# The last strip's rows summed and turned one piece sooner, and a weight split held back, behind an output norm

## What is computed

```python
m = jnp.concatenate([a, p], axis=-1) @ w_o[l]
x = x + rms_norm_2(m, post_mix_g[l])
h = rms_norm_2(x, pre_ffn_g[l])
up = causal_dwconv(h @ w_up[l], conv_w[l], conv_b[l])
y = (jax.nn.gelu(up[..., :D_FF_2], approximate=True) * up[..., D_FF_2:]) @ w_down[l]
x = x + rms_norm_2(y, post_ffn_g[l])
```

## Time and profile before

| | |
|---|---|
| median of 3 runs | 2122.08 us (2122.01 to 2123.68) |
| profiled execution, its own time | 2123.21 us |
| its span (first to last instruction) | 2121.5 us |
| TensorE busy | 2112.6 us (100%) |
| VectorE, ScalarE, GpSimd busy | 1255.2 us, 1051.7 us, 190.1 us |
| weight load (beside the matmuls) busy | 1812.9 us |
| DMA | 194 GB/s in the mean |

### The profile page before, as it was taken

How to read it: one execution, slowest core, us unless ns; L and a number is a source line. 1 busy time by engine, 2 the same in 40 slices (tenths; PEclk the granted TensorE clock), 3 DMA queues, 4 the chain that set the end, 5 groups by cost and what they waited for, 6 DMA issues and landing times.

```text
span 2121.5 us, 26812 instructions
## 1 busy us (share of the span) xinstructions
PE 2112.6 (100%) x11014; PEld 1812.9 (85%) x11014; DVE 1255.2 (59%) x1337; ACT 1051.7 (50%) x1224; POOL 190.1 (9%) x90
## 2 busy tenths in 40 slices
PE   9999999999999999999999999999999999999998
PEld 8888888888888888888888888888888888888887
DVE  6555656656455555465667755576666644666565
ACT  6654555544334443344555645465455433455543
POOL 3000000000000000000004000002222100222210
PEclk9999999999999999999999999999999999999999
DMA  8565557665666666665676656655655666556663
GB/s 288 166 209 174 179 169 231 221 197 174 209 195 184 196 209 194 182 195 193 219 237 189 187 171 196 192 183 174 193 191 181 212 195 189 182 176 203 202 208 120
DMA packets 218923, 411.98 MB, mean 194 GB/s; under 512 B 13360, under 2 KB 22704, under 8 KB 218288
## 3 DMA queue, kind: packets, MB, share of 16 engines
q1 hardware_dynamic: 217936, 405.77, 60.5%
q10 hardware_dynamic: 864, 4.49, 0.6%
HBM read 403.92 MB, written 6.29 MB: 193 GB/s over the span
## 4 chain that ended last, share of the span: by engine, by line
PE 98%; DMA 1%; DVE 0%; ACT 0%; issue 0%; SPq 0%; DVEq 0%
PE ps L1491 98%; DMA xT<-in_x_dram 0%; DMA E<-passed_rows 0%; PE ps L1494 0%; DMA passed_rows<-xN 0%; DVE aHL L1248 0%; DVE xN L1258 0%; DVE T L1237 0%; SPq L858 0%; DVE Wl L1141 0%; ACT aHL L944 0%; DVE aHL L1241 0%; SPq L863 0%; ACT T L1070 0%; DVE Wl L1137 0%
## 5 line engine op out<-in xcount | busy, mean ns | idle before, releaser
L1141 DVE TENSOR_TENSOR Wl<-raw,Wh 128x1024 fp32r<-128x1024 f32 x743 | 911.4, 1246 | 648.3 <-ACT Wh L920 647.6
L1491 PE MATMUL ps<-aHL,Wh 128*128 128x512 f32 x3336 | 1159.1, 392 | 1.6 <-DVE Wl L1137 1.0
L920 ACT ACTIVATE Wh<-raw 128x1024 fp32r<-128x1024 f32 x743 | 767.4, 1054 | 583.3 <-PE ps L1491 580.7
L1491 PE MATMUL ps<-aHL,Wl 128*128 128x256 f32 x3328 | 930.1, 280 | 0.0
L1491 PEld LDWEIGHTS ps<-aHL,Wh 128*128 128x128 f32 x3336 | 623.9, 187 | 140.7 <-issue 1.1
L1491 PEld LDWEIGHTS ps<-aHL,Wl 128*128 128x128 f32 x3328 | 628.3, 189 | 0.5
L1491 PE MATMUL ps<-Wh,hid 128*128 128x512 f32 x1728 | 532.6, 389 | 0.0
L1491 PEld LDWEIGHTS ps<-Wh,hid 128*128 128x128 f32 x1728 | 324.3, 188 | 67.4
L1491 PE MATMUL ps<-Wl,hid 128*128 128x512 f32 x864 | 336.2, 389 | 0.0
L1491 PEld LDWEIGHTS ps<-Wl,hid 128*128 128x128 f32 x864 | 162.2, 188 | 33.6
L1491 PE MATMUL ps<-Wh,oHL 128*128 128x512 f32 x512 | 158.8, 390 | 0.0
(11 more groups left out here) (177 smaller groups left out, 796.2 us busy)
## 6 DMA issues: line engine op xcount, KB each, us to landing
raw<-in_mlp_w_dram SPq DMA_DIRECT2D x256, 512.0 KB, 4.2
raw<-in_w_up_dram SPq DMA_DIRECT2D x176, 512.0 KB, 3.7
raw<-in_sb_w_qkv_dram SPq DMA_DIRECT2D x93, 512.0 KB, 4.8
raw<-in_w_down_dram SPq DMA_DIRECT2D x88, 512.0 KB, 4.2
raw<-in_w_in_dram SPq DMA_DIRECT2D x64, 512.0 KB, 4.6
raw<-in_sb_w_o_dram SPq DMA_DIRECT2D x32, 512.0 KB, 5.3
raw<-in_w_o_dram SPq DMA_DIRECT2D x32, 512.0 KB, 4.3
passed_rows<-xN SPq DMA_DIRECT2D x16, 256.0 KB, 4.3
```

The lines of the kernel that those rows point to most:

```text
L920: e.activation(Wh[:, i % NW, :], rawv[:, i % NRAW, :], ACT.Copy).then_inc(st["hi"][0], 1)
L1141: e.tensor_tensor(Wl[:, i % NW, :], rawv[:, i % NRAW, :], Wh[:, i % NW, :].bitcast(F32), ALU.subtract).then_inc(st["lo"][0], 1)
L1491: return e.matmul(o, l, r, start=start, stop=stop, skip_group_check=True)
```

## The change

Two things are edited. In `evac_mixed`, `add_rows(3)` and `move_rows(3)` no longer stand in the put-off job `second_tiles` (iteration of piece 0), but in the evacuation itself, right behind `keep_last`, one iteration sooner. `turn_blocks` is put off by three iterations from there, so it also comes one iteration sooner, behind piece 2 and not behind piece 3; there it is registered ahead of `tiles(2)`. And the split that iteration 0 of the strip emitted (that of piece 4) moves to iteration 1.

```diff
@@ -498,11 +498,11 @@
             add_rows(1)
             p.pieces[p.at + 1]["early"] = dict(hi=st["t_hi"], lo=st["t_lo"], turning=tiles(0, (2, 3)))
             step("keep_last", set=s, row=st["mixed_row"], kept=kept[1])
+            add_rows(3)
+            move_rows(3, "ffn", added[3] * 2)
 
             def second_tiles():
                 tiles(1)
-                add_rows(3)
-                move_rows(3, "ffn", added[3] * 2)
                 add_rows(2)
             later(1, second_tiles)
             later(3, lambda: tiles(2))
@@ -678,7 +678,7 @@
     for i in range(N):
         q = p.pieces[i]
         p.at = i
-        while n_split <= (i + LEAD if i > 2 else i + 1):
+        while n_split <= (i + (LEAD - 1 if q["early"] else LEAD) if i > 2 else i + 1):
             split(n_split)
             n_split += 1
         need = []
```

## The result

| | median, us | lowest to highest | ratio to before, 95% interval |
|---|---|---|---|
| before, 8 runs | 2122.51 | 2122.0 to 2123.68 | |
| changed, 8 runs | 2128.66 | 2127.91 to 2129.74 | 1.0029 (1.0021 to 1.0038) |

The change makes the kernel 6.15 us, 0.29%, slower: clear of the 0.2% bound, if only just. Predicted were 2127.3 us, in a range from 2124.2 to 2130.2. The profiled execution of the changed kernel took 2127.91 us, its span is 2126.2 us, and its mean granted clock 0.998.

A forecast was written before the change was run, and what follows sets the result against it. TensorE bounds the kernel, busy 2112.6 of 2121.5 us, so only its waits and clock matter. +4.35 (wait) - 0.36 (old wait gone) + 1.2 (clock) = +5.2 us on 2122.08 gives 2127.3 us, range 2124.2 to 2130.2.

The forecast's parts named there:

- What the change can win: TensorE's wait for L1241 before piece 6, for tiles 12 and 13, goes away: 0.36 us saved.
- The order of the jobs as the cause: On ScalarE and VectorE the blocks' job now comes ahead of turning tiles 8 to 11, which delays piece 4: 4.35 us.
- The wait: TensorE before piece 4 waits for tiles 8 and 9: it starts at 1399.8 in place of 1395.45, 4.35 us.
- T: Start of the transposition L1237 on VectorE, which waits for the moved rows: 5.4 us after the first issue, 1395.4.
- piece 4 at T + 4.4: TensorE starts piece 4 4.4 us after the transposition starts, behind the blocks' halves and those of tiles 8 and 9.
- The clock: Clock falls 3.4 us into TensorE's wait; 2.4 us of matmuls at half speed lose 1.2 us, bounds 0 and 3.4.
- The held split: Piece 4's weight split comes later, ready at 1391.4 and wanted at 1395.45: covered by pieces 1 to 3, cost nothing.
- The sum ahead of tiles 4 and 5: On VectorE, low halves of tiles 4 and 5 still end before piece 2 wants them: cost nothing, 0.9 us to spare.
- The load behind the rows on SyncE: Piece 10's load goes out at about 1391.9, not 1386.96; its split waits past 1401 anyway: cost nothing.
- The clock that holds: Rival: TensorE's wait before piece 4 comes, but the clock doesn't fall: +4.0 us, 2126.1 us; chance 0.33.
- The quick transfer: Rival: rows land sooner, transposition at 1393.8, TensorE waits 2.75 us before piece 4: +2.4 us, 2124.5 us; chance 0.14.
- The other side: Rival: tiles 8 to 11 ready by 1395.45, no new wait, only 0.36 us saved: 2121.7 us; chance 0.08.

The follow-up runs named there:

- both reorderings: Two kernels, each the change with one edit: turning of tiles 8 to 11 registered ahead of the blocks (2122.63 us), or the blocks put behind piece 3 again (2122.48 us).
- the held split alone: The kernel before with only the changed `while` line, which holds back piece 4's weight split by one piece: 2122.79 us, before 2122.72, ratio 1.0001.
- the runs with the loads held: The change, with SyncE waiting until the moved rows have landed before it issues the next weight loads: 2129.04 us, before 2122.53; one more profiled execution took 2130.01.
- the runs with matmuls of ones: Matmuls of ones into an unused bank ahead of piece 4's wait: the change with 34 (2129.95 us) or 19 (2127.10), only the transposition ahead with 8 (2124.43).
- the move alone: The change with the old `while` line, so without holding back piece 4's split: 2130.47 us, before 2122.72, ratio 1.0042; a second, single profiled run took 2128.64 us.
- the change again: The change itself, unedited, timed and profiled a second time: 2130.10 us, before 2122.53, ratio 1.0033.
- the run with 19 matmuls of ones: The change, with 19 matmuls of ones into an unused bank just ahead of TensorE's wait for piece 4: 2127.10 us, before 2122.61, ratio 1.0022.
- only the transposition ahead: The change, with only the blocks' transposition ahead of tiles 8 to 11 and the blocks' high and low halves behind them: 2125.02 us, before 2122.53, ratio 1.0013.

## Why the prediction was right

**What the change can win: 0.36 us.** Right by the traces: the wait for L1241 is gone in the change, in both reorderings and with the held split alone. As a time it is too small to be seen: the medians of the last three kernels differ from before by 0.1 to 0.2 us, in both directions.

**The order of the jobs as the cause.** Right. Swapping the two jobs takes the whole loss away; the other edits of the change left in place cost nothing, and the held split left out saves nothing.

**The wait: 4.35 predicted, 4.54 measured** in the profile. Both its parts fit: T at 5.4 after the first read (5.45), piece 4 at T + 4.4 (4.39). The second is sound working, built from two rows for each engine. The first was half luck. The step "nearer to this strip's own 6.03 than to 4.14, but under it, since the second load behind it now waits for one more split" gives the loads behind the transfer as its reason, and the runs with the loads held don't bear that out: 5.03 and 5.06 us with no load behind. With loads behind, the profiles in which VectorE waited gave 4.06, 5.06, 5.19, 5.26, 5.29, 5.31, 5.40, 5.45, 5.72 and before 6.03 for this strip. So most of the length is there without loads; whether they widen the spread two profiles can't tell. What sets the slowest read, and so the spread, is open.

**The clock: 1.2 predicted, 1.56 in the profile, 1.7 to 3.1 in the medians.** The mechanism was right, and the runs with matmuls of ones show it as a cost of its own. The size was too small: the term let the fall come 3.4 us after TensorE stopped, as at the end of the kernel before, and so the first microsecond of the low level pass within the wait. In the change's profile the fall came 4.3 us after TensorE stopped, 0.07 us before the wait's end, so nearly all 3.4 us hit matmuls. Over the six profiles in which it fell here it came from 2.5 us (the loads held) to 5.2 us (the change again) after the stop, so one row could not time it. The low level, for whose length the prediction had no row and assumed another 3.4 us, lasted 3.4 us in four of the six; in the two with the loads held it lasted 6.8 us, the first 1.5 us of them within the wait, and cost 2.5 us, inside that step's bound of 3.4.

**The sum.** 4.54 - 0.36 + 1.56 = 5.7 us by the one profile, 6.15 by the medians, 5.2 predicted. The 1.4 us between 2127.3 and 2128.66 are 0.4 us by which the kernel before is slower in eight runs (2122.51) than in the three that the prediction had (2122.08), 0.2 of the wait, 0.4 of the clock, and 0.4 that the profile's terms don't show. With the 7.6 us of the change's second timing, that last part grows to 1.9 us: the terms account for the quickest executions and not fully for the median one.

**The free parts.** The held split: free, no wait for L1141. The sum ahead of tiles 4 and 5: free, with 0.8 us to spare (their low halves end at 1386.9, piece 2 starts at 1387.72; 0.9 predicted), which one more split uses up, as the move alone shows. The load behind the rows on SyncE: no wait for it anywhere.

**The rivals.** The clock that holds is what the run with 19 matmuls of ones makes of the change, and it lands at +4.5 where the rival had +4.0. The quick transfer occurred in one profile, that of the move alone, as an execution and not as the rule; and there the clock fell all the same, behind a wait of 2.6 us, which that rival's +2.4 left out (six pairs from 1399.24 took 3.64 us in place of 2.12). That rival drew the transfer from the quickest slice's landing, 2.4 us after its issue. The Trainium skill's fixed cost pointed the same way (the Trainium skill, DMA: Bandwidth & Descriptors, "Anatomy of one DMA"); that section states it for transfers that GpSimd issues, and these are SyncE's. Even with no load behind it the move took 5.03 us from its first issue, against some 3.7 by that reckoning, an estimate. The other side was excluded by the order itself.

## What to carry to other kernels

When a job is moved sooner, look at what it is put ahead of, on every engine that has a part in it: here 0.36 us stood to be won, and a job that waits for a transfer was put in front of tiles that were ready and due sooner. In a list of work for engines that run in order, sort by when the inputs are there and when the result is due, not by when the job can be issued. And price a wait of TensorE of some microseconds at more than its length: the clock may fall in it, or just behind it.

## What the runs showed that was not expected

- The clock also falls after a wait that is already over. In the change's second profile it fell 0.9 us after the wait. In the first profile of the move alone TensorE stood for 2.6 us, ran four pairs at full speed (the last three 0.35 us each), and then went to 0.64 us a pair from 1399.24 on, 1.5 us after it had resumed:

```profile
1397.76 0.47 PE L1491 MATMUL ps<-aHL,Wh 128*128 128x512 f32 x1 [2.55 <-DVE aHL L1248]
...
1399.24 0.63 PE L1491 MATMUL ps<-aHL,Wh 128*128 128x512 f32 x1
```

- The time at the low level was 3.4 us in the two profiles of the change and the two of the move alone, and 6.8 us in both with the loads held, after waits that differ from the change's by 0.4 us only. A longer wait does not mean a longer low level.
- A wait of 2.0 us left the clock alone in the one execution that was profiled, that of only the transposition ahead.
- An fp32 matmul of ones leaves two records of 0.11 us in the profile (34 of them left 68, in 7.5 us): count by time, not by the number of records.
